# A two-layer hybrid decoder trunk: one split of the feed-forward and one of the output projection in another place in ScalarE's order

## The reference

```
x = x + 0.5 * swiglu(rms_norm(x, ffn1_norm), w_gate, w_up, w_down)     # width 2816
x = x + hybrid_mixer(rms_norm(x, mix_norm), ...)                       # three token mixers
x = x + 0.5 * swiglu(rms_norm(x, ffn2_norm), w_gate, w_up, w_down)

swiglu(h) = (silu(h @ w_gate) * (h @ w_up)) @ w_down
hybrid_mixer: y = sigmoid(gate_a) * (o_a @ w_branch[0]) + sigmoid(gate_b) * (o_b @ w_branch[1])
                + sigmoid(gate_c) * (o_c @ w_branch[2]);  return y @ w_out
```

## Time and profile before

| | |
|---|---|
| median of 3 runs | 2781.63 us (2776.05 to 2782.74) |
| the profiled execution's own time | 2779.79 us |
| its span, first to last instruction | 2778.0 us |
| mean granted TensorE clock | 0.995 of full speed |
| PE busy | 2692.3 us, 97% of the span |
| POOL, DVE, ACT busy | 1079.9, 1281.1, 941.1 us |

### The profile page before, as it was taken

One profiled execution on the slowest core, in us unless ns is written; L12 is line 12 of the kernel. 1 busy time (PEld: TensorE's weight loads), 2 busy tenths in 40 slices (PEclk: granted clock), 3 DMA queues, 4 the chain that ended last, 5 costly groups with the idle time before them and its releaser, 6 DMA issues.

```text
span 2778.0 us, 37033 instructions
## 1 busy us (share of the span) xinstructions
PE 2692.3 (97%) x13220; PEld 2148.7 (77%) x13220; DVE 1281.1 (46%) x1600; ACT 941.1 (34%) x1431; POOL 1079.9 (39%) x450
## 2 busy tenths in 40 slices
PE   7999999999998999999999999999999999999999
PEld 5888887776776787888878888877667777878887
DVE  6333353466457365332353333534664663743323
ACT  4222232655533333222142222335554334332221
POOL 4444444421322344444444444444122224444443
PEclk9999999999999999999999999999999999999999
DMA  3222223211111222223222222233011112322232
GB/s 141 91 106 108 87 92 102 105 47 39 58 60 55 80 106 96 91 94 116 82 88 91 101 101 100 86 104 106 32 43 64 57 58 83 106 96 91 94 114 79
DMA packets 36183, 239.54 MB, mean 86 GB/s; under 512 B 4065, under 2 KB 5345, under 8 KB 14049
## 3 DMA queue, kind: packets, MB, share of 16 engines
q1 hardware_dynamic: 34112, 233.85, 23.8%
q10 hardware_dynamic: 1952, 4.12, 0.4%
HBM read 234.81 MB, written 2.10 MB: 85 GB/s over the span
## 4 chain that ended last, share of the span: by engine, by line
issue 61%; POOL 25%; PE 12%; POOLq 1%; DMA 0%; DVE 0%; ACTq 0%; ACT 0%; DVEq 0%
POOL wlo L289 25%; PE bank L1245 4%; PE bank L1247 4%; PE bank L1246 4%; POOLq L288 1%; POOLq L284 1%; DMA x<-xT 0%; DVE hlo L716 0%; DVE x L786 0%; DVE hhi L714 0%; POOLq L289 0%; POOL vcm L273 0%; POOL selr L274 0%; ACTq L298 0%; ACT L295 0%
## 5 line engine op out<-in xcount | busy, mean ns | idle before, releaser
L289 POOL TENSOR_TENSOR wlo<-raw,whi 128x1024 fp32r<-128x1024 f32 (+2 forms) x440 | 1078.3, 2452 | 1684.1 <-ACT whi L321 796.7
L1245 PE MATMUL bank<-hhi,whi 128*128 128x512 f32 x1968 | 789.8, 401 | 32.7 <-POOL wlo L289 26.3
L1247 PE MATMUL bank<-hhi,wlo 128*128 128x512 f32 x1968 | 770.6, 392 | 0.0
L1246 PE MATMUL bank<-hlo,whi 128*128 128x512 f32 x1968 | 769.8, 391 | 0.0
L312 ACT ACTIVATE whi<-raw 128x1024 fp32r<-128x1024 f32 (+1 forms) x232 | 263.8, 1138 | 715.7 <-PE bank L1247 715.7
L1245 PEld LDWEIGHTS bank<-hhi,whi 128*128 128x128 f32 x1968 | 372.2, 189 | 121.0 <-issue 32.4
L1247 PEld LDWEIGHTS bank<-hhi,wlo 128*128 128x128 f32 x1968 | 371.3, 189 | 78.2
L1246 PEld LDWEIGHTS bank<-hlo,whi 128*128 128x128 f32 x1968 | 372.4, 189 | 73.1 <-issue 2.4
L773 DVE TENSOR_TENSOR tmp<-tmp,bank 128x512 f32<-128x512 f32 x80 | 55.1, 688 | 534.0 <-PE bank L1247 534.0
L1245 PE MATMUL bank<-uhi,whi 128*128 128x512 f32 x704 | 274.7, 390 | 0.0
L1247 PE MATMUL bank<-uhi,wlo 128*128 128x512 f32 x704 | 274.3, 390 | 0.0
(11 more groups left out here) (296 smaller groups left out, 3039.2 us busy)
## 6 DMA issues: line engine op xcount, KB each, us to landing
raw<-gu SPq DMA_DIRECT2D x88, 1024.0 KB, 4.7
raw<-dn SPq DMA_DIRECT2D x32, 1408.0 KB, 6.0
raw<-cb SPq DMA_DIRECT2D x48, 768.0 KB, 4.2
raw<-pM SPq DMA_DIRECT2D x16, 1024.0 KB, 4.8
raw<-cq SPq DMA_DIRECT2D x16, 1024.0 KB, 4.8
raw<-pA SPq DMA_DIRECT2D x12, 1024.0 KB, 4.7
raw<-wo SPq DMA_DIRECT2D x8, 1024.0 KB, 4.7
x<-xT ACTq DMA_DIRECT2D x4, 512.0 KB, 7.5
```

The source lines that it names most:

```text
L289: pool.tensor_tensor(wlo[:, s, 0:w], raw[:, j, lo:lo + w], whi[:, s, 0:w].bitcast(f32), ALU.subtract).then_inc(sem["lo_done"], 1)
L1245: mm(outp, wh, mhi, start=start and k == 0, stop=False)
L1246: mm(outp, wh, mlo, start=False, stop=False)
L1247: i = mm(outp, wl, mhi, start=False, stop=stop and k == len(parts) - 1)
```

## The change

In the feed-forwards `norm` issues the split of tile 6 (the first tile of the fourth unit) directly behind the two SiLUs of line 379, ahead of the wait for `uhi_ready`, of the parameter load and of the SiLU of the third unit. `section` gets a flag `begun`, with which only tile 7 is split at its old place. This holds for all four starts.

At the end of cb2 the copies y_high(5) and y_high(6) stand ahead of the last turn. In that turn the gate of unit 7 is taken ahead of the split of the second tile of wo. On DVE y_low(5) and y_low(6) stand ahead of the combination of unit 7. PE, POOL and SP have the same instructions as before.

```diff
@@ scalar engine
-                def section(name, extra=None, first=0):
+                def section(name, extra=None, first=0, begun=False):
...
                     unit(first, 0, split=False)
-                    unit(first, 1)
+                    if begun:
+                        split_tile(name, 4 * first + 3)
+                    unit(first, 1, split=not begun)
...
                             A(tmp[:, j], tmp[:, j], ACT.Silu).then_inc(sem["silu_ready"], 1)
+                        split_tile(begins, 6)
                         act.wait_ge(sem["uhi_ready"], me.at("uhi_ready", f // 2 * KF + 2))
...
-                section("gu0", silu, first=1)
+                section("gu0", silu, first=1, begun=True)
...
                     act.wait_ge(sem["tile_done"], me.at("tile_done", 2 * u + 2))
-                    A(whi[:, 1, 0:w], raw[:, 1 - j, w:2 * w], ACT.Copy).then_inc(sem["hi_done"], 1)
+                    if not last:
+                        A(whi[:, 1, 0:w], raw[:, 1 - j, w:2 * w], ACT.Copy).then_inc(sem["hi_done"], 1)
                     act.wait_ge(sem["y_ready"], me.at("y_ready", 2 * KD + c - 1))
                     A(tmp[:, j], bank[2 * j][:], ACT.Tanh, ...).then_inc(sem["gate_ready"], 1)
+                    if last:
+                        A(whi[:, 1, 0:w], raw[:, 1 - j, w:2 * w], ACT.Copy).then_inc(sem["hi_done"], 1)
...
                 y_high(KD - 4)
-                turn(KD // 2 - 1, 1, last=True)
-                y_high(KD - 3)
-                for k in (KD - 2, KD - 1):
+                for k in (KD - 3, KD - 2, KD - 1):
+                    if k == KD - 1:
+                        turn(KD // 2 - 1, 1, last=True)
                     act.wait_ge(sem["y_ready"], me.at("y_ready", 2 * KD + k + 1))
                     y_high(k)
...
-                section("gu1", silu, first=1)
+                section("gu1", silu, first=1, begun=True)
@@ vector engine
-                with dve.Fori(1, KD // 2) as i:
+                with dve.Fori(1, KD // 2 - 1) as i:
                     for j in range(2):
                         combine_unit(2, j, FIRST["cb2"] + j + 2 * i, 2 * i + j)
                         y_low(2 * i + j - 2)
-                for k in (KD - 2, KD - 1):
+                combine_unit(2, 0, FIRST["cb2"] + KD - 2, KD - 2)
+                for k in (KD - 4, KD - 3, KD - 2):
                     y_low(k)
+                combine_unit(2, 1, FIRST["cb2"] + KD - 1, KD - 1)
+                y_low(KD - 1)
```

## The result

The changed kernel took 2765.55 us (median of 4 runs, 2764.61 to 2766.40) against 2782.18 for the kernel before (2776.05 to 2789.22): a ratio of 0.9934, 95% interval 0.9922 to 0.9947. Applied to the 2781.63 us with which I started, the ratio gives 2763.3. I had forecast 2769.4, range 2764 to 2776. The kernel is faster, as forecast, but by 16.6 us between the medians, or 18.4 by the ratio, where I had 12: at the low end of the range, and by the ratio just outside it. Three more comparisons of the same two kernels, further down (a3, c4, d3), gave 15.3, 18.4 and 12.8 us, so the size is best taken as about 16 us. One execution of the kernel before, in group d, took 3091 us at a granted clock of 0.826 and is left out of every comparison and mean.

What follows compares the result with a forecast made beforehand. PE, busy 97% of the span, was taken as the bound, so only its gaps could give time. Feed-forward 11.3 us (3.2 clock) plus output projection 0.0: 2779.79 + 0.9 - 11.3 = 2769.4 us, range 2764 to 2776.

Steps and rivals of the forecast that it cites:

- the 0.2 us that I had left there: At gu1, tile 7 was forecast ready at 1070.4 to 1070.8, due at 1070.98: it fits with 0.2 to spare.
- the end that I took: At the moved split, POOL gets in behind DVE's rounding, is done at 54.6, and the gap at tile 6 goes whole.
- the rival in which it stands back: POOL stands back behind DVE at all four feed-forward starts; gain 8.9 us, time 2771.8; chance 0.18.
- the two low stretches of one profile: Feed-forward matmuls at PE's lower clock behind the gaps at 1068.42 and 2446.19; removing them gives 3.2 us.
- The rival that had the clock pay the gain back: Two or three more low-clock stretches elsewhere take 3 to 5 us, leaving 2773 to 2775, no change; chance 0.14.
- each gap at the length of one execution: Feed-forward waits at tile 6 were added up from the gaps of one profile, within a sum of 11.3 us.
- POOL 0.03 ahead: In wo's first tile, POOL's subtraction starts at 987.94, DVE's addition for y[7] at 987.97: called a tie, POOL first.
- a gain of 0: Output projection: PE's wait moves to the eighth step and stays 1.5 us; ends -0.1 and +0.7 per layer, 0 taken.
- the start of line 834: DVE's addition for y[7] in the output projection, put at 987.97: 0.22 behind the gate, then 0.85 behind line 830.
- the nearest row that I leaned on: Row at 1016.36, where DVE's operation 0.06 us behind POOL's had to wait; used to judge the output-projection tie.
- DVE wins the tie: Rival: DVE's addition for y[7] precedes POOL in the output projection, 0.7 us per layer, time 2768.0; chance 0.14.
- the two readings in the prediction: At moved split: by the port rule POOL enters after one DVE instruction, full 11.3; by row 44.75 it's held, lower end.

Runs made afterwards that it cites:

- a3: The changed kernel once more, nothing altered, against the kernel before on the same chip: 2766.09 us, ratio 0.9945.
- c4: The changed kernel once more, as base for the candidate's runs, against the kernel before: 2764.62 us, ratio 0.9934.
- d3: The changed kernel again, beside the repeated candidate on one chip, against the kernel before: 2767.68 us, ratio 0.9954.
- group d: The last set of runs, kernels d1, d2 and d3 on one chip, each with the kernel before beside it.
- a1: Only the feed-forward part of the change (split of tile 6 moved in all four starts), against the kernel before: 2765.32 us, ratio 0.9946.
- c1: Changed kernel plus a 256-column DVE clear between product and addition for y[7]: 2764.80 us, ratio 0.9934 to before; changed kernel beside it 2764.62.
- b4: Changed kernel with DVE's last pair of combinations put back into a loop of one pass: 2769.69 us, ratio 0.9948 to the kernel before.
- c2: Changed kernel with the gate of unit 7 behind the split of wo's second tile again: 2765.42 us, ratio 0.9935 to the kernel before.
- c3: Changed kernel with gu0's split of tile 5 between the two SiLUs, waiting for DVE's sixth low part: 2760.52 us, ratio 0.9920 to the kernel before.
- d1: Changed kernel plus a 512-column DVE clear between product and addition for y[7]: 2766.02 us, ratio 0.9949 to before; changed kernel beside it 2767.68.
- d2: The candidate again: changed kernel with gu0's split of tile 5 deferred: 2762.62 us, ratio 0.9941 to before; changed kernel beside it 2767.68.
- b1: Split of tile 6 moved only in the two gu1 starts, against the kernel before: 2773.47 us, ratio 0.9970.
- b3: Split of tile 6 behind the wait for DVE's second product, ahead of parameter load and third SiLU, against the kernel before: 2774.38 us, ratio 0.9972.
- a2: Only the output-projection part of the change, feed-forwards as before, against the kernel before: 2777.25 us, ratio 0.9989.

## Why the prediction was right or wrong

**Right: where the time was and who held it.** ACT's wait for DVE's second product held the split of tile 6. With the split ahead of it the wait at tile 6 is gone in every one of the 24 changed starts that a1, the changed kernel in its four profiles and c1 have (four each), and in the 20 of b4, c2, c3, d1 and d2; b1 to b3 give the dose. None of the 44 shows a wait at tile 7 either, with the 0.2 us that I had left there. POOL got in between DVE's products, the end that I took; the rival in which it stands back, and with it 2771.8, is out.

**Right in kind, too small: the clock.** I had counted the two low stretches of one profile, 3.2 us. In the profiles 10 of 16 unchanged starts were followed by one, 2 x (7/8 + 3/8) = 2.5 per execution, which at 1.6 us each is 4.0 us. The granted clocks point the same way, with less weight: their mean is 0.9939 over the 75 executions of the kernel before in the groups a to d and 0.9955 over the changed kernel's 20. If PE were busy throughout, 0.16% of 2780 us would be 4.4 us. But among executions of the same kernel 0.001 of clock goes with only 1.3 us, not 2.8, and by that the term is 2.1. So it lies between 2.1 and 4.4 us, an estimate. The rival that had the clock pay the gain back fell: the total went the other way. In single profiles it does move: low stretches of four or more matmuls number 7 and 12 in the two of the kernel before, 6, 9, 4 and 7 in the four of the changed one. The first gap of gu0's tile 4, 2 us in all of them, was followed by the lower clock in some only: not in the first profile of before, but in the first of after.

**Too small: the waits in the feed-forward.** The step that failed was to take each gap at the length of one execution. The two outcomes of POOL against DVE at tile 5 make 8.0 us of mean gap where I had 7.3, so about 8.9 for the waits where I had 8.1.

**Wrong: the output projection.** I took "POOL 0.03 ahead" and a gain of 0. The runs show DVE 0.18 ahead, a wait of 0.36 instead of 1.38 us, with no scatter in it: both layers of a2 and of the changed kernel's later profiles have 0.36 too. The step that failed here, and the only one that left a whole term at nothing, is the start of line 834, put at 0.22 and 0.85 behind its predecessors from the loop's rows, though the diff takes this pair out of the loop. Also the nearest row that I leaned on has POOL at an idle DVE, which says nothing on a DVE already at work. The rival "DVE wins the tie" was the case that came, with 1.0 us per layer where I had priced it at 0.7: against that rival's own sum y[7] was ready 0.25 us earlier, and POOL was through 0.4 us earlier. How far the tie itself matters is open: in c1 and d1 DVE came later than in the changed kernel and still wasn't held (waits of 0.45 and 0.71). Over two layers PE's rows give 2 x 1.02 = 2.0 us, a2's ratio 3.1 (0.6 to 5.3).

Summed again: 8.9 (waits) + 2.1 to 4.4 (clock) + 2.0 (output projection) = 13.0 to 15.3 us; with the 4.0 of the counted stretches it is 14.9. The means of those 75 and 20 executions, 2781.3 and 2765.8, are 15.5 apart. So the three terms carry most of the gain, and up to 2.5 us of it may have a source that was not found.

**The page's rule.** The Trainium skill, page "SBUF — State Buffer", section "SBUF: two separate sides", has the port change hands by whole instructions, the first come first. In the trace it does change hands within DVE's chain of eight in most starts (2.8 us for the subtraction), but in some POOL stands behind the whole chain (6.45 us), and in d1 an addition that came 0.24 us behind POOL went first. With no gap between DVE's instructions the rule doesn't say who is next, and here either happened. Of the two readings in the prediction, at the moved split of tile 6 the rule's was the one that came: POOL was let in there, in 2.4 to 3.0 us, in all 44 starts.

## What to carry to other kernels

Ahead of a wait in an engine's stream, put what doesn't depend on it; here one copy per section, moved over one wait, gave most of the gain without any new work. A gap's length in one profile is one draw where two engines contend for a port: look at every repetition of the stage, and take a second profile before adding up. Take the distance between operations from rows of the same form: a pair moved out of a loop started its second operation 0.2 us sooner here, as much as the margin on which my forecast of a tie rested.

## What the runs showed of the hardware that I had not expected

The same chain of eight DVE subtractions (4.9 us alone) and one POOL subtraction (2.4 alone), with POOL coming 0.64 to 0.70 us behind the chain's start, end in two ways: DVE 4.89 and POOL 6.45 us, or DVE 7.06 and POOL 2.80. The distance doesn't tell them apart (0.70 occurs with both). Of the 30 profiled gu0 starts that split tile 5 at the old place, 4 ended in the first way, two of them in the one profile that the prediction was read from, and 24 in the second. In the other two, in b1 and d1, POOL came only 4.4 us behind the chain's start, the chain took 8.1 us, and PE waited 0.8 us in tile 4.

A loop of one pass (b4) left DVE's distances at 0.11 and 0.73 us, those of operations written out, where a loop of several passes has 0.22 and 0.85.
